# Gate projections of a three-layer stack: one weight load for both activation halves, blocks of 256 channels, the forget-gate attention's gate multiplied later

## The chip, the cores and the metric

The kernel runs on one NeuronCore of one Trainium2 chip. The metric is the device time of one execution in microseconds. All arrays lie in HBM before the start and the result is written back there.

## The reference

A stack of three layers over 256 tokens of width 2048, in float32. Layers 0 and 1 share one form. Each modulates and normalises `x` to `u`, projects `u` with `w_in` (2048 by 19064), runs three branches and merges them. What matters here, cut down:

```python
proj = jnp.dot(u, w_in)
(fq, fk, fv, ff, fg, dq, dk, dv, iq, ik, iw, dg, sz, sxbc, sdt, mg) = jnp.split(proj, ...)
y_fox = fox_attention(fq, fk, fv, log_f).reshape(B, S, FOX_WIDTH) * jax.nn.silu(fg)
y_dsa = dsa_attention(dq, dk, dv, iq, ik, iw).reshape(B, S, DSA_WIDTH) * jax.nn.silu(dg)
y_ssd = ...            # state-space branch, times silu(sz), grouped rms_norm
gates = jax.nn.sigmoid(mg.reshape(B, S, 3, D) + b_merge)
merged = (gates[:, :, 0] * jnp.dot(y_fox, w_o_fox) + gates[:, :, 1] * jnp.dot(y_dsa, w_o_dsa)
          + gates[:, :, 2] * jnp.dot(y_ssd, w_o_ssd))
x = x + gate[:, None, :] * jnp.dot(merged, w_out)
# third layer (layer 2 in the kernel)
y_a = h.astype(x.dtype) * jax.nn.silu(g_lru)
y_b = windowed_gqa(q, k, v, sink) * jax.nn.silu(g_attn)
```

The gate blocks of the title are the projections to `fg` and `dg` (1024 channels each, in layers 0 and 1) and to `g_lru` and `g_attn` (2048 channels each, in layer 2).

## The kernel before

**Products.** Each large product is done with float32 operands split in a high part and a low part: `UH`, `UL` for `u`; `HH`, `LL` for a piece of weights. Three products are summed in PSUM: high by high, low activation by high weight, high activation by low weight. A piece of weights is 1 MB (128 partitions by 2048 words), called a chunk. Its way is: a DMA to one of the `RAW` buffers; `hi` on ScalarE (L1511), which writes `HH`; `lo` on VectorE (L1875), which writes `LL` over the RAW buffer; then the products on TensorE (L1277). There are 3 `HH` buffers, so `hi` of chunk g waits until the products of chunk g - 3 are done, and ScalarE, which works strictly in order, waits with it.

**Blocks.** A block is 512 output channels, that is 4 chunks of 4 k-tiles of 128 rows. Blocks use two sets of two PSUM banks in turn (set 0: `G0`, `G1`; set 1: `G2`, `G3`), so block n + 2 can begin only when block n is evacuated. There are two kinds. In kind `tm` (tokens by channels) the activations are the loaded operand and 512 columns of weights stream: 24 matmuls of 512 columns a chunk. In kind `cm` (channels by tokens) the weights are loaded and 256 columns of activations stream: 48 matmuls of 256 columns a chunk. The profile names a matmul by the streamed operand and then the loaded one, `G<-UH,HH`. The gate blocks are `cm`: 4 blocks each in layers 0 and 1 and 8 in layer 2, 16 in all.

**Order.** `work_order` makes one list of tokens, and each engine's program walks it and takes its own. After the products of each chunk it calls `slot`, which takes one step of the side lane (attention, state-space scan, recurrences, tables for the next layer) and one step of the evacuation lane (a first-in-first-out queue of block evacuations and of the splits of `y` into `YH`, `YL`). If the block about to start needs a set whose last block has no evacuation step yet, `gemm` calls `slot` again until it has, with no products in between; what is put then stands behind the `hi` of the chunk two places further on. A block marked `ahead` has the pending `lo` put before its evacuation step. Chunks are numbered in this order; chunks 93 to 100 are the `fg` blocks of layer 0, 294 to 297 the last four of them in layer 1.

**Gates.** A gate block's evacuation is `silu` (two tokens, one a bank): ScalarE takes tanh of the bank into `S1` (L1617), VectorE makes (tanh + 1) times the bank (L2062) and multiplies this into the attention's or recurrence's result, `QQ` or `XS` (L2069). It is held until that result is there. Before `fg` come four `sz` blocks, whose evacuation takes more steps: `sz_gate` (tanh on ScalarE L1655, two operations on VectorE L2100 and L2103, once for each bank), `sz_norm` (L1659, L1661, L2109, L2111), a turn on TensorE (L1372) and `sz_put` (L2116). After the `fg` blocks come the gates of the merge (`gate`, L2127 and L1675), the splits (L1690, L2156) and, in layer 1, tables of layer 2: `rope` (L1917 to L1939, sine L1552) and `lru_par` (L2195 to L2258, L1732, L1735). `ada` is a dot product on VectorE (L1886, two of 128x1024).

## Time and profile before

| | |
|---|---|
| time, median of 3 runs | 3382.77 us (3380.96 to 3383.23) |
| profiled execution, first to last instruction | 3380.1 us |
| median less that span (start and end around it) | 2.7 us |
| TensorE busy | 3279.9 us, 97% of the span |
| VectorE busy | 2253.8 us, 67% |
| ScalarE busy | 1690.3 us, 50% |
| mean granted clock of TensorE | 0.992 |

A row of a timeline reads: start in us from the span's start, duration, engine, line, operation, output <- inputs, count; in brackets the idle time of that engine before it and what ended it. PE is TensorE, DVE is VectorE, ACT is ScalarE. A matmul's duration is its time through the array; consecutive ones overlap, so what a matmul costs in a stream is the distance from its start to the next start.

### The profile page before, as it was taken

Reading aid. Unit: us, or ns where it says so; the run is one execution under the profiler, and the core shown is the slowest. Engines: PE = TensorE matmul, PEld = TensorE weight load, DVE = VectorE, ACT = ScalarE, POOL = GpSimd, SP = SyncE. Lnnn points to the kernel's source line nnn. Section 1 sums busy time; section 2 is a strip of 40 time slices with the busy share of each in tenths; the row PEclk is TensorE's granted clock in tenths of the full one; section 3 lists DMA queues with packets and bytes.
Section 4 is the critical chain, followed back from the end, with each engine's and each line's share of the span. In section 5 each row is a group of like instructions: output and inputs, shape, how many; then the busy total and the mean of one; then the engine's idle time right before and its main releaser. Section 6 shows DMA issues by size and latency. Waiting matters only on the chain.

```text
span 3380.1 us, 43397 instructions
## 1 busy us (share of the span) xinstructions
PE 3279.9 (97%) x17994; PEld 2845.1 (84%) x17994; DVE 2253.8 (67%) x2699; ACT 1690.3 (50%) x2090; POOL 46.8 (1%) x90
## 2 busy tenths in 40 slices
PE   4899999999999999999999999999999999999998
PEld 3789889888888878898898888888798899988887
DVE  7878878866676556786666676655577776544454
ACT  4455764643433445556646544334447865434343
POOL 0000000000000000000000000000000000000000
PEclk8999999999999999999999999999999999999999
DMA  9854566567777654444544577765545443455554
GB/s 403 325 187 174 200 252 252 197 232 273 270 278 277 227 206 175 175 152 175 185 175 164 185 264 268 277 220 190 196 183 191 181 165 131 174 213 198 188 188 147
DMA packets 102916, 719.29 MB, mean 213 GB/s; under 512 B 12176, under 2 KB 12256, under 8 KB 18752
## 3 DMA queue, kind: packets, MB, share of 16 engines
q1 hardware_dynamic: 93888, 675.38, 54.0%
q0 software_dynamic: 8256, 37.64, 3.1%
q8 instruction: 142, 2.33, 0.3%
q10 hardware_dynamic: 576, 3.50, 0.3%
q14 instruction: 54, 0.44, 0.0%
HBM read 710.08 MB, written 6.40 MB: 212 GB/s over the span
## 4 chain that ended last, share of the span: by engine, by line
PE 88%; DVE 7%; DMA 2%; ACT 2%; issue 1%; DVEq 0%; ACTq 0%
PE G L1277 81%; DVE LL L1875 2%; DMA RAW<-w_ada_turned_packed_dram 2%; PE BD L1389 1%; DVE S L2079 1%; PE BA L1416 1%; DVE RAW L1868 1%; PE BD L1451 1%; DMA KV<-in_x_dram 1%; PE BC L1402 0%; PE BE L1332 0%; DVE RAW L1886 0%; PE BA L1470 0%; PE BC L1470 0%; PE BC L1434 0%
## 5 line engine op out<-in xcount | busy, mean ns | idle before, releaser
L1511 ACT ACTIVATE HH<-RAW 128x2048 fp32r<-128x2048 f32 x546 | 1044.8, 1914 | 1096.7 <-PE G L1277 1019.1
L1875 DVE TENSOR_TENSOR LL<-RAW,HH 128x2048 fp32r<-128x2048 f32 x546 | 1248.0, 2287 | 370.5 <-ACT HH L1511 370.0
L1277 PE MATMUL G<-HH,UH 128*128 128x512 f32 x2496 | 994.2, 398 | 35.1 <-DVE LL L1875 23.4
L1277 PE MATMUL G<-LL,UH 128*128 128x512 f32 x2496 | 977.0, 391 | 0.0
L1277 PE MATMUL G<-HH,UL 128*128 128x512 f32 x2496 | 976.7, 391 | 0.0
L1277 PE MATMUL G<-UH,HH 128*128 128x256 f32 x2080 | 602.0, 289 | 5.7 <-DVE LL L1875 5.6
L1277 PE MATMUL G<-UH,LL 128*128 128x256 f32 x2080 | 588.8, 283 | 0.0
L1277 PE MATMUL G<-UL,HH 128*128 128x256 f32 x2080 | 588.7, 283 | 0.0
L1277 PEld LDWEIGHTS G<-HH,UH 128*128 128x128 f32 x2496 | 471.7, 189 | 137.4 <-DVE LL L1875 26.1
L1277 PEld LDWEIGHTS G<-LL,UH 128*128 128x128 f32 x2496 | 471.4, 189 | 100.4
L1277 PEld LDWEIGHTS G<-HH,UL 128*128 128x128 f32 x2496 | 471.7, 189 | 97.9 <-issue 2.9
L1277 PEld LDWEIGHTS G<-UH,HH 128*128 128x128 f32 x2080 | 398.9, 192 | 12.2 <-DVE LL L1875 8.0
L1277 PEld LDWEIGHTS G<-UL,HH 128*128 128x128 f32 x2080 | 399.2, 192 | 1.8 <-issue 1.0
L1277 PEld LDWEIGHTS G<-UH,LL 128*128 128x128 f32 x2080 | 398.9, 192 | 0.0
L1277 PE MATMUL G<-HH,YH 128*128 128x512 f32 x768 | 299.9, 391 | 0.0
L1277 PE MATMUL G<-LL,YH 128*128 128x512 f32 x768 | 299.0, 389 | 0.0
L1277 PE MATMUL G<-HH,YL 128*128 128x512 f32 x768 | 298.8, 389 | 0.0
L1277 PEld LDWEIGHTS G<-LL,YH 128*128 128x128 f32 x768 | 144.2, 188 | 30.1
L1277 PEld LDWEIGHTS G<-HH,YH 128*128 128x128 f32 x768 | 144.2, 188 | 29.9 <-DVE LL L1875 0.3
L1277 PEld LDWEIGHTS G<-HH,YL 128*128 128x128 f32 x768 | 144.2, 188 | 29.7
L1886 DVE SCALAR_TENSOR_TENSOR RAW<-RAW,CH 128x1024 f32<-128x1024 f32 x128 | 151.3, 1219 | 0.0
L2079 DVE SCALAR_TENSOR_TENSOR S<-G,PAR,S 128x253 f32<-128x253 f32 x144 | 69.3, 481 | 42.5 <-ACT S L1631 38.2
(387 smaller groups left out, 2329.0 us busy)
## 6 DMA issues: line engine op xcount, KB each, us to landing
RAW<-in_w_in_packed_dram SPq DMA_DIRECT2D x402, 1024.0 KB, 4.8
RAW<-w_ada_turned_packed_dram SPq DMA_DIRECT2D x96, 1024.0 KB, 5.0
RAW<-in_w_out_packed_dram SPq DMA_DIRECT2D x48, 1024.0 KB, 4.8
...
```

The lines of the kernel that those rows point to most:

```text
L1277: mm = pe.matmul(to, lt, rh, start=first, stop=end, skip_group_check=True)
L1389: mm = pe.matmul(BD[:, j * P:(j + 1) * P], vt[:, t, vof(h + j):vof(h + j) + P], W[3][:, (j * nt + t) * P:(j * nt + t + 1) * P], start=t == ...
L1416: mm = pe.matmul(to, QQ[:, h + j, qt * P:(qt + 1) * P], kt[:, kof(h + j), 0:nk], start=True, stop=True)
L1451: pe.matmul(BD[:, j * 64:(j + 1) * 64], W[j // 4][:, (j % 4) * P:(j % 4 + 1) * P], XD[:, j * 64:(j + 1) * 64], start=True, stop=True)
L1511: a.activation(HH[g % NH][:, :n], RAW[buf(ch["f"])][:, :n], ACT.Copy).then_inc(*hi_done.up(g))
L1868: v.scalar_tensor_tensor(RAW[buf(f)][:, :], RAW[buf(f)][:, :], 0.5, CB[:, :], ALU.mult, ALU.mult, accum_out=DOT[:, 0, c:c + 1]).then_inc(* ...
L1875: v.tensor_tensor(LL[buf(f)][:, :n], RAW[buf(f)][:, :n], HH[g % NH][:, :n].bitcast(F32), ALU.subtract).then_inc(*lo_done.up(g))
L1886: done = v.scalar_tensor_tensor(r, r, 0.5, CH[:, :], ALU.mult, ALU.mult, accum_out=DOT[:, e["half"], c:c + 1])
L2079: v.scalar_tensor_tensor(to, of, weight(j), to, ALU.mult, ALU.add).then_inc(*done.up(*key, n))
```

## The change

A gate block is now 256 channels: 2 chunks of 8 k-tiles (`wide`). `UH` and `UL` become the two halves of one tile `UU`, side by side for each k-tile. For each k-tile and each 128 channels there are two matmuls instead of three on each 256 columns: the high weights are loaded once and stream 512 columns, high and low activations, into the whole bank; the low weights stream the 256 high columns into its first half. The sum of the two halves of the bank is then left to the evacuation. This `sg` copies the first half to SBUF on ScalarE, adds the second half on VectorE (this frees the bank), takes tanh of the sum on ScalarE and multiplies on VectorE. A second token, `sm`, multiplies by the result of the attention or recurrence. For `dg`, `gl` and `ga` `sm` follows `sg`; for `fg` the gates stay in `BT` and `CTT` (free once the state-space branch is done) and `times_late` multiplies them after all four blocks.

```diff
+    def wide(self, w, c0, evac, ready, **kw):
+        chunks = []
+        for kc in range(KT // 8):
+            src = (*w, kc * 1024, 1024, [(c0, 256)])
+            parts = [("ab", j, 0, j * P, P, 0) for j in range(2)]
+            chunks.append({"src": src, "w": 256, "nk": 8, "k0": kc * 8, "parts": parts})
+        return self.block(chunks, evac, ("U", 0), ready, KT, **kw)
...
+    def silu_gate(key, prog):
         def steps(b):
             o.tok_block[key] = b
-            for j in range(2):
-                put("silu", key, j)
+            put("sg", key)
+            o.blocks[b]["free_by"] = ("sg_sum", key)
+            ended("sg_silu", key)
+            yield
+            yield from times(key, prog)
+        return steps
+
+    def silu_early(key, prog):
+        def steps(b):
+            o.tok_block[key] = b
+            while not prog["done"]:
                 yield
-            ended("silu_done", key, 1)
+            put("sg", key)
+            o.blocks[b]["free_by"] = ("sg_sum", key)
+            ended("sg_silu", key)
+            yield
         return steps
...
-        for j in range(2):
-            o.wblock(w, DG + j * 512, o.held(o.att_prog["dsa", l][j], silu_times(("dg", l, j))), u_ready, ahead=True)
+        for j in range(4):
+            o.wide(w, DG + j * 256, silu_gate(("dg", l, j), o.att_prog["dsa", l][j // 2]), u_ready, ahead=True)
...
-            add_to(s_fd, [split(("y", l, i)) for i in range(4)])
+            add_to(s_fd, [times_late(l)] + [split(("y", l, i)) for i in range(4)])
...
-        for j in range(2):
-            o.wblock(w, FG + j * 512, o.held(o.att_prog["fox", l][j], silu_times(("fg", l, j))), u_ready, ahead=True,
-                     after=after_fg if j else None)
+        for j in range(4):
+            o.wide(w, FG + j * 256, silu_early(("fg", l, j), o.ssd_prog[l][3]), u_ready, ahead=True,
+                   after=after_fg if j == 3 else None)
...
-    UH = sb("UH", [P, KT, S], F32R)
-    UL = sb("UL", [P, KT, S], F32R)
+    UU = sb("UU", [P, KT, 2, S], F32R)
+    UH, UL = UU[:, :, 0, :], UU[:, :, 1, :]
...
-                for j in range(3):
+                for j in range(2 if kind == "ab" else 3):
...
+                    if kind == "ab":
+                        w_ = (hv, lv)[j]
+                        end = kk == b["kts"] - 1 and j == 1
+                        to = GB[b["set"]][bi][:, 0:(512, S)[j]]
+                        lt, rh = w_[:, k, c0:c0 + P], (UU[:, kk, :, :].rearrange("p a b -> p (a b)"), UH[:, kk, :])[j]
...
+            for j in range(2):
+                i = a.activation(g[:, j, :], GB[o.blocks[b]["set"]][j][:, 0:S], ACT.Copy)
+            i.then_inc(*sg_copied.up(key))
+            a.wait_ge(*sg_sum.at(key))
+            a.activation(th, g, ACT.Tanh, scale=0.5).then_inc(*sg_tanh.up(key))
...
+            for j in range(2):
+                i = v.tensor_tensor(g[:, j, :], g[:, j, :], GB[o.blocks[b]["set"]][j][:, S:2 * S], ALU.add)
+            i.then_inc(*sg_sum.up(key))
+            v.wait_ge(*sg_sum.at(key))
+            v.wait_ge(*sg_tanh.at(key))
+            v.scalar_tensor_tensor(g, th, 1.0, g, ALU.add, ALU.mult).then_inc(*sg_silu.up(key))
```

**Place 1, ScalarE, layer 0, from the `hi` of chunk 96 on.** `HH` numbers are the chunk number modulo 3; `L1655` is the tanh of `sz_gate`, here of the last `sz` block. Before:

```order
L1511 ACTIVATE HH0<-RAW0 128x2048
L1511 ACTIVATE HH1<-RAW1 128x2048
L1655 ACT_TABLE_LOAD
L1655 ACTIVATE S1<-G2 128x512
L1511 ACTIVATE HH2<-RAW3 128x2048
L1655 ACTIVATE XD<-G3 128x512
L1659 ACTIVATE S1,SM2<-XS 128x512
```

Now (the lines are 52 to 57 further down: L1563 is `hi`, L1712 the tanh of `sz_gate`, L1671 and L1674 the copies and the tanh of `sg`):

```order
L1563 ACTIVATE HH0<-RAW0 128x2048
L1563 ACTIVATE HH1<-RAW1 128x2048
L1712 ACT_TABLE_LOAD
L1712 ACTIVATE S1<-G2 128x512
L1712 ACTIVATE XD<-G3 128x512
L1716 ACTIVATE S1,SM2<-XS 128x512
L1718 ACT_TABLE_LOAD
```

Both `sz_gate` steps now stand directly behind the `hi` of chunk 97, and TensorE's chunk 95, the first of the second `fg` block, which takes `G2` and `G3`, waits for both; before, chunk 95 was in the middle of a block that already had its banks.

**Place 2, VectorE, layer 0, a little later.** `L1886` and `L1944` are `ada`, `L2116` and `L2180` are `sz_put`, `LL` rows are `lo`. Before, up to the first `silu` of `fg`, which the chunk after the `fg` blocks waits behind:

```order
L2116 TENSOR_TENSOR XS<-BE,PAR 128x512
L1875 TENSOR_TENSOR LL1<-RAW1,HH2 128x2048
L1875 TENSOR_TENSOR LL2<-RAW2,HH0 128x2048
L2062 SCALAR_TENSOR_TENSOR S1<-S1,G0 128x512
L2069 SCALAR_TENSOR_TENSOR QQ<-S1,QQ 128x512
L1875 TENSOR_TENSOR LL4<-RAW4,HH1 128x2048
L2062 SCALAR_TENSOR_TENSOR S1<-S1,G1 128x512
L2069 SCALAR_TENSOR_TENSOR QQ<-S1,QQ 128x512
```

Now (L1933 is `lo`, L2118 the add of `sg`):

```order
L1944 SCALAR_TENSOR_TENSOR RAW2,DOT<-RAW2,CH 128x1024 x2
L2180 TENSOR_TENSOR XS<-BE,PAR 128x512
L1933 TENSOR_TENSOR LL3<-RAW3,HH2 128x2048
L2180 TENSOR_TENSOR XS<-BE,PAR 128x512
L1933 TENSOR_TENSOR LL4<-RAW4,HH0 128x2048
L2118 TENSOR_TENSOR BT<-BT,G0 128x256
L2118 TENSOR_TENSOR BT<-BT,G1 128x256
L2122 SCALAR_TENSOR_TENSOR BT<-S1,BT 128x512
```

The adds that free `G0` and `G1` for chunk 97 (the third `fg` block) stand behind the `lo` of chunk 99 (`LL4<-RAW4,HH0`), whose `hi` waits for the end of chunk 96. The wait at the end of the `fg` blocks, behind `LL4<-RAW4,HH1` (chunk 103) in the rows of before, has gone: there the adds stand two blocks earlier.

**Place 3, ScalarE, layer 1, after the `fg` blocks.** `YH<-QQ` are the four splits, `ROWS` and `SPL` the two steps of `lru_par`, `WW` the tanh of the first merge gate. Before:

```order
L1511 ACTIVATE HH2<-RAW5 128x2048
L1735 ACT_TABLE_LOAD
L1735 ACTIVATE SPL<-PAR 128x32
L1690 ACTIVATE YH<-QQ 128x1024
L1511 ACTIVATE HH0<-RAW0 128x2048
L1690 ACTIVATE YH<-QQ 128x1024
L1511 ACTIVATE HH1<-RAW2 128x2048
L1690 ACTIVATE YH<-QQ 128x1024
L1675 ACT_TABLE_LOAD
L1675 ACTIVATE WW<-WW 128x512 x2
L1511 ACTIVATE HH2<-RAW3 128x2048
```

Now (L1748 the split, L1793 `SPL`, L1732 the tanh of the merge gate):

```order
L1563 ACTIVATE HH0<-RAW0 128x2048
L1790 ACT_TABLE_LOAD
L1790 ACTIVATE ROWS<-ROWS 128x32
L1748 ACTIVATE YH<-QQ 128x1024
L1563 ACTIVATE HH1<-RAW2 128x2048
L1793 ACT_TABLE_LOAD
L1793 ACTIVATE SPL<-PAR 128x32
L1748 ACTIVATE YH<-QQ 128x1024 x2
L1732 ACT_TABLE_LOAD
L1732 ACTIVATE WW<-WW 128x512 x2
L1563 ACTIVATE HH2<-RAW3 128x2048
```

Behind the `hi` of chunk 304 (`HH1<-RAW2`) stood one split and the gate's tanh; now `SPL`, two splits and the gate's tanh stand there.

## Rows read from the trace of the kernel before

**Rows 1.** The page: busy time, then the chain that ended last.

```profile
PE 3279.9 (97%) x17994; PEld 2845.1 (84%) x17994; DVE 2253.8 (67%) x2699; ACT 1690.3 (50%) x2090; POOL 46.8 (1%) x90
...
PE 88%; DVE 7%; DMA 2%; ACT 2%; issue 1%; DVEq 0%; ACTq 0%
```

**Rows 2.** Timeline of TensorE inside a `cm` chunk: first and 48th matmul.

```profile
530.02 0.28 PE L1277 MATMUL G<-UH,HH 128*128 128x256 f32 x1
...
535.66 0.28 PE L1277 MATMUL G<-UH,LL 128*128 128x256 f32 x1
```

**Rows 3.** Timeline of TensorE in a `tm` chunk: first and 20th matmul shown.

```profile
2219.63 0.39 PE L1277 MATMUL G<-LL,YH 128*128 128x512 f32 x1
...
2223.94 0.39 PE L1277 MATMUL G<-HH,YH 128*128 128x512 f32 x1
```

**Rows 4.** Timeline of TensorE at the end of `fg`, layer 0.

```profile
723.55 0.28 PE L1277 MATMUL G<-UH,LL 128*128 128x256 f32 x1
729.63 0.77 PE L1277 MATMUL G<-HH,UH 128*128 128x512 f32 x1 [5.80 <-DVE QQ L2069]
...
732.72 0.40 PE L1277 MATMUL G<-HH,UL 128*128 128x512 f32 x1
```

**Rows 5.** The same place: timelines of ScalarE (one row) and VectorE.

```profile
723.93 1.91 ACT L1511 ACTIVATE HH<-RAW 128x2048 fp32r<-128x2048 f32 x1 [1.93 <-PE G L1277]
...
725.87 2.29 DVE L1875 TENSOR_TENSOR LL<-RAW,HH 128x2048 fp32r<-128x2048 f32 x1 [2.13 <-ACT HH L1511]
...
728.79 0.69 DVE L2069 SCALAR_TENSOR_TENSOR QQ<-S,QQ 128x512 f32<-128x512 f32 x1
```

**Rows 6.** Timeline of TensorE, layer 1: the same wait, and the one after the splits.

```profile
1916.79 0.77 PE L1277 MATMUL G<-HH,UH 128*128 128x512 f32 x1 [5.80 <-DVE QQ L2069]
...
1952.56 0.50 PE L1277 MATMUL G<-HH,UH 128*128 128x512 f32 x1 [0.98 <-DVE LL L1875]
```

**Rows 7.** `sz_gate` of the last `sz` block, layer 0: timelines of ScalarE and VectorE.

```profile
688.47 1.92 ACT L1511 ACTIVATE HH<-RAW 128x2048 fp32r<-128x2048 f32 x1 [4.27 <-PE G L1277]
690.40 1.28 ACT L1655 ACT_TABLE_LOAD   x1
691.70 0.60 ACT L1655 ACTIVATE S<-G 128x512 f32<-128x512 f32 x1
...
693.05 0.69 DVE L2103 SCALAR_TENSOR_TENSOR XS<-S,XS 128x512 f32<-128x512 f32 x1
```

**Rows 8.** By line: a copy and an operation near 256 columns, and `ada`.

```profile
L1760 ACT ACTIVATE QQ<-BD x48: 358/384/385, 379.5 to 2906.1; 128x256 f32<-128x256 f32 x48
...
L2079 DVE SCALAR_TENSOR_TENSOR S<-G,PAR,S 128x253 f32<-128x253 f32 x144 | 69.3, 481 | 42.5 <-ACT S L1631 38.2
...
L1886 DVE SCALAR_TENSOR_TENSOR RAW<-RAW,CH 128x1024 f32<-128x1024 f32 x128 | 151.3, 1219 | 0.0
```

**Rows 9.** Timelines of layer 1 after `fg`: ScalarE, then VectorE.

```profile
1940.65 1.92 ACT L1511 ACTIVATE HH<-RAW 128x2048 fp32r<-128x2048 f32 x1 [1.00 <-PE G L1277]
1943.22 1.06 ACT L1690 ACTIVATE YH<-QQ 128x1024 fp32r<-128x1024 f32 x1 [0.66 <-DVE YL L2156]
...
1940.27 0.17 DVE L2205 TENSOR_SCALAR PAR<-PAR 128x32 f32<-128x32 f32 x1
...
1941.97 1.22 DVE L2156 SCALAR_TENSOR_TENSOR YL<-QQ,YH 128x1024 fp32r<-128x1024 f32 x1
1943.11 2.29 DVE L1875 TENSOR_TENSOR LL<-RAW,HH 128x2048 fp32r<-128x2048 f32 x1
...
1950.22 2.28 DVE L1875 TENSOR_TENSOR LL<-RAW,HH 128x2048 fp32r<-128x2048 f32 x1
```

**Rows 10.** Stretch with `dg` blocks, layer 0: PE, PEld, DVE, ACT, POOL busy.

```profile
540.00:560.00 20.00, 20.00 (x165) 19.52 (x165) 17.64 (x24) 8.10 (x11) 0.00 (x0) 1.00 0.69 259
```

**Rows 11.** Layer 2, after a `ga` evacuation: timelines of VectorE and TensorE.

```profile
2910.89 2.28 DVE L1875 TENSOR_TENSOR LL<-RAW,HH 128x2048 fp32r<-128x2048 f32 x1
...
2914.49 0.28 PE L1277 MATMUL G<-UH,HH 128*128 128x256 f32 x1
```

More of the change, by code:

```diff
@@ L429, in tokens, with times, times_late @@
         return steps
-    def silu_times(key):
+    def silu_gate(key, prog):
         def steps(b):
             o.tok_block[key] = b
-            for j in range(2):
-                put("silu", key, j)
+            put("sg", key)
[8 more added lines that the diff above has]
+            while not prog["done"]:
                 yield
-            ended("silu_done", key, 1)
-        return steps
+            put("sg", key)
+            o.blocks[b]["free_by"] = ("sg_sum", key)
+            ended("sg_silu", key)
+            yield
+        return steps
+    def times(key, prog):
+        while not prog["done"]:
+            yield
+        put("sm", key)
+        ended("sm_done", key)
+        yield
+    def times_late(l):
+        for j in range(4):
+            while not o.att_prog["fox", l][j // 2]["done"]:
+                yield
+            put("sm", ("fg", l, j))
+            ended("sm_done", ("fg", l, j))
+            if j % 2:
+                yield
     def conv(l, jb):
@@ L795, in work_order @@
     o.side.add(o.when(qkv_b, attention("att2", 2)))
-    for j in range(4):
-        o.wblock(w, 2048 + j * 512, o.held(lru_prog[j], silu_times(("gl", 2, j))), u_ready2)
+    for j in range(8):
+        o.wide(w, 2048 + j * 256, silu_gate(("gl", 2, j), lru_prog[j // 2]), u_ready2)
     s_a, s_b, s_u2 = [], [], []
@@ L805, in after_gates @@
         add_to(s_a, [split(("a", 2, i)) for i in range(4)] + [bring(2)])
-    for j in range(4):
-        o.wblock(w, 7168 + j * 512, o.held(o.att_prog["att2", 2][j], silu_times(("ga", 2, j))), u_ready2,
-                 after=after_gates if j == 3 else None)
+    for j in range(8):
+        o.wide(w, 7168 + j * 256, silu_gate(("ga", 2, j), o.att_prog["att2", 2][j // 2]), u_ready2,
+               after=after_gates if j == 7 else None)
     branch(2, 0, w, 9216, ("w_proj_a_2", 0), 0, 16, lambda kk: ("split_lo", ("a", 2, kk // 4)), s_a, u_ready2,
@@ L1046, in hybrid_stack @@
     dv_copied = count("dv_copied", [(h[1], t) for h, t in o.all("hd") if h[0] == "dk"])
-    silu_tanh = count("silu_tanh", o.all("silu"))
-    silu_done = count("silu_done", o.all("silu"))
+    sg_copied, sg_sum = count("sg_copied", o.all("sg")), count("sg_sum", o.all("sg"))
+    sg_tanh, sg_silu = count("sg_tanh", o.all("sg")), count("sg_silu", o.all("sg"))
+    sm_done = count("sm_done", o.all("sm"))
     sz_tanh, sz_y = count("sz_tanh", o.all("sz_gate")), count("sz_y", o.all("sz_gate"))
@@ L1567, in u @@
                 a.wait_ge(*u_full.at(l, pi))
[L1568 removed]
+                a.activation(UH[:, 2 * pi:2 * pi + 2, :], SS[pi % 2][:, :].rearrange("p (a b) -> p a b", a=2),
+                             ACT.Copy).then_inc(*u_hi.up(l, pi))
         def gate_cols(l):
@@ L2053, in hd, with sg, sm @@
                 rotated.append((h, t))
-        def silu(key, j):
+        def sg(key):
             b = o.tok_block[key]
-            bk = GB[o.blocks[b]["set"]][j]
-            dst, c0 = silu_dst[key[0]]
-            c0 += key[2] * 4 + 2 * j
-            d = flat(dst[:, c0:c0 + 2, :])
-            v.wait_ge(*silu_tanh.at(key, j))
-            v.scalar_tensor_tensor(S1[:, :], S1[:, :], 1.0, bk[:, :], ALU.add, ALU.mult).then_inc(*own.up())
-            v.wait_ge(*own.last())
+            g, th = gate_tiles(key)
+            v.wait_ge(*sg_copied.at(key))
+            for j in range(2):
[4 more added lines that the diff above has]
+            v.scalar_tensor_tensor(g, th, 1.0, g, ALU.add, ALU.mult).then_inc(*sg_silu.up(key))
+        def sm(key):
+            dst, c0 = silu_dst[key[0]]
+            d = dst[:, c0 + 2 * key[2]:c0 + 2 * key[2] + 2, :]
+            v.wait_ge(*sg_silu.at(key))
             if key[0] == "gl":
-                v.wait_ge(*lru_done.at(key[2] * 4 + 3))
+                v.wait_ge(*lru_done.at(2 * key[2] + 1))
             else:
                 name = {"dg": "dsa", "fg": "fox", "ga": "att2"}[key[0]]
-                v.wait_ge(*att_y.at(name, key[1], key[2] * 4 + 3))
-            v.scalar_tensor_tensor(d, S1[:, :], 0.5, d, ALU.mult, ALU.mult).then_inc(*silu_done.up(key, j))
+                v.wait_ge(*att_y.at(name, key[1], 2 * key[2] + 1))
+            v.scalar_tensor_tensor(d, gate_tiles(key)[0], 0.5, d, ALU.mult, ALU.mult).then_inc(*sm_done.up(key))
         def taps(done, main, key, ps, dst, weight, shifts):
```

36 lines of the change are left out of this document (21 added, 15 removed).

## The prediction, written before the changed kernel was run

> **What bounds the kernel now.** The page comes first: TensorE is busy 97% of the span and holds 88% of the chain that ended last, while VectorE has 67% and ScalarE 50% [rows 1]. So a change pays in two ways only: cheaper matmul streams, or fewer and shorter holes on TensorE. For the streams I read TensorE's timeline. Inside a `cm` chunk 48 starts lie between 530.02 and 535.66, 0.120 us apart [rows 2]; in a `tm` chunk 20 starts span 4.31 us, 0.227 us apart [rows 3]. At 2.4 GHz, the level of both stretches, 256 columns are 0.1067 us and 512 are 0.2133 us, so a matmul with its load costs its columns and 0.0133 us more, at either size. For the holes I read the same timeline at the ends of blocks. The largest inside the layers stands at the end of `fg`: last start at 723.55, next at 729.63, 5.96 us more than a step of the stream, and again in layer 1 [rows 4, 6]. The row names VectorE's `QQ` as what ended it. The chain back is: end of chunk 100, `hi` at 723.93 (0.38 us after that last start), `lo` at 725.87, the two `silu` operations until 729.48, TensorE 0.15 us later [rows 5]. After it the clock is at its lower level until 732.72: seven matmuls take 3.09 us where the stream needs 1.59, a loss of 1.5 us [rows 4].
>
> **The streams.** The 16 gate blocks hold 16 x 4 chunks x 48 = 3072 matmuls of 256 columns. They become 1024 of 512 and 1024 of 256 columns. The columns are the same; 1024 matmuls and loads go, at 0.0133 us each: -13.7 us. A chunk takes 16 x 0.347 = 5.55 us instead of 5.76. No row shows a 256-column matmul between two of 512 with other weights, so the bounds are: nothing saved, if the extra time comes back where the sizes alternate, and twice the row, -27 us, if the 256-column ones also lose theirs. I take the row's figure, as both sizes show the same excess.
>
> Here a page speaks against the gain. The Trainium skill, "TensorE: Matmul & The Clock Gate" (section "Wait — 56ns, not 53.3ns?"), says that back-to-back matmuls at full clock start their columns at 2.4 GHz plus about 2.5 ns apart. By that floor the 1024 removed would give 2.6 us and the sum below would be +23.7, where the row gives +12.6. The rows differ from it: 13.3 ns here, with a load before each matmul, and the row decides.
>
> **The old hole.** The adds of the last `fg` blocks stand early enough, so 5.96 us go in each of two layers: -11.9 us. Its clock loss goes with it, and comes back below.
>
> **New hole A** (place 1 of the change), both layers. The `fg` blocks are half as long, but the evacuation of the last `sz` block needs as many steps. Chunk 95 is now the first of a block that needs the banks of that `sz` block, and both `sz_gate` steps stand behind the `hi` of chunk 97, which waits for the end of chunk 94. From the last start of chunk 94: `hi` at +0.38; by the spacings of rows 7 table load at +2.31, first tanh at +3.61, second operation of VectorE at +4.96, ending at +5.65; the second bank's tanh is done by then, its two operations take 0.69 each and 0.03 between, to +7.06; TensorE at +7.21, 7.1 us beyond a step [rows 5, 7]. Nothing hides it: the next products need that bank. 2 x 7.1 = +14.2 us. The clock will fall as after the old hole: 2 x 1.5 = +3.0 us.
>
> **New hole B** (place 2), both layers. Chunk 97 waits for the adds of the first `fg` block, behind the `lo` of chunk 99, whose `hi` waits for the end of chunk 96. `hi` +0.38 to +2.30, `lo` to +4.6, two adds of 256 columns. The nearest row for one is an operation of 253 columns at 0.481 us, between nothing (an add hidden in the wait) and 0.69 us, that of 512 columns [rows 5, 7, 8]; I take 0.45, so +5.5, TensorE at +5.65: 5.5 us each, +11.0 us. Its clock loss replaces that of the old hole.
>
> **Hole C** (place 3), layer 1. Before, chunk 304 started 1.1 us late at 1952.56, as soon as its `lo` of 1950.22 had ended [rows 6, 9]; that `lo` stands behind the merge gate's two adds and an `ada`. Counted from the end of chunk 301 (about 1940.3) the chain was: `hi` 304, third split's low part with a `lo` of 2.29 us behind it, last split, add, `ada` (2.44), add, `lo`. Now that `lo` is ahead of the chain, but in it come the third split's high part (1.05) and low part (1.22), a table load (1.28) with the small steps of `lru_par` (0.3 before the split, and 1.70 as between 1940.27 and 1941.97) [rows 7 to 9]. In order: `hi` to +2.2, table +3.5, `SPL` +4.2, high part +5.2, low +6.4, `lru_par` +8.1, low part of the last split +9.3, add +10.1, `ada` +12.4, add +13.0, `lo` +15.3. Two `tm` chunks last 10.9, so chunk 304 is 4.4 us late by that. ScalarE and VectorE also come later to this point, since the sines and an `ada` now stand behind the last `sg`: counted in the same way from the start of chunk 298 (add, tanh, two `lo`, two `sm`, `ada`, sines at 2.5 and 2.0 us, estimated from the ten small steps), `lo` of chunk 302 ends at +23.2 where TensorE wants it at +21.9, 1.3 us late, and the `hi` of 304 and VectorE's own `lo` of 303 come about 1.4 us late against the products. Sum 7.1 us against 1.1: +6.0 us, and a loss of clock, +1.5 us. If all of `lru_par` hides in idle time this is +2.
>
> **VectorE in `dg` of layer 0.** A 512-channel pair of blocks costs VectorE 4 adds x 0.45 and 4 operations x 0.69, 4.6 us, against 2.7 before; so +3.6 us for the four blocks, and each `sg` waits about 0.7 us for ScalarE's tanh (0.60) besides: 6.4 us in all over eight chunks, some 48 us. VectorE has 2.4 us idle in 20 there, so 5.7 in that time [rows 8, 10]. It becomes the limit: the 1.7 us that these chunks save are lost and about 0.5 more: +2.2 us. In layer 1 and elsewhere VectorE has room.
>
> **Layer 2.** With no attention beside it, the `lo` two chunks on followed a `ga` evacuation at 2910.89 and ended at 2913.17, 1.3 us before its matmul at 2914.49 [rows 11]. `sg` is longer by one copy step and the wait for tanh, about 1 us, and the chunk is 0.2 shorter: the margin is 0.1 us. I count +0.3 us for all of it. ScalarE's copies are 0.38 us each against a tanh of 0.60 and hide [rows 7, 8].
>
> **Sum:** -13.7 - 11.9 + 14.2 + 3.0 + 11.0 + 7.5 + 2.2 + 0.3 = +12.6 us. The profiled span is 3380.1 us, with 2.7 us around it to the median of 3382.77: the span becomes 3392.7 and the time 3395.4, 0.37% slower. What a measurement of this kernel can tell from no change is about 0.2%, 6.8 us: 3376.0 to 3389.6.
>
> **Rivals.**
> *The holes are shallow (same).* If the clock does not fall at A and C and C costs 2 us, the sum is 12.6 - 3.0 - 5.5 = +4.1: 3387 us. For it: a hole of 5.96 us cost 1.5, not more, and phases vary. Against it: both old holes of that length show the loss. Chance 0.18.
> *The loads are worth more (faster).* If the 13 ns go from the 256-column matmuls too, -27 instead of -13.7, the time is 3382; with shallow holes as well 3374, faster. With my holes it turns at a saving of 33 us. For it: no row of mixed sizes. Against: both sizes carry the same excess. Chance of both together: 0.05.
> *VectorE becomes the limit in layer 2 as well (slower still).* If each of the 16 wide blocks there loses 1 us because margins of 1.3 us are too short, +16: 3411 us. It decides from 1.3 us of added delay at each `sg`. Against: beside attention a chunk lasts longer and margins are wider. Chance 0.12.
> *The streams give little (slower still).* If the excess over the columns belongs to a change of weights that cannot be hidden, and the alternation of sizes costs it again, 2.6 us or less come instead of 13.7: 3406 us. For it: no row alternates. Against: the excess is the same behind 256 and 512 columns. Chance 0.07. The page named above gives this time.
> *The change costs nothing and gives the loads alone.* If A does not stand where the order puts it, 3395.4 - 14.2 - 3.0 = 3378. Against: bank and order are fixed in the program. Chance 0.05.
>
> **Numbers.** Forecast as summed 0.53, own range 3390 to 3401. Faster: the 0.05 of the load rival and 0.02 from the rival without hole A, 0.07. Same: 0.18 and the other 0.03, less 0.01 that ends above 3389.6, 0.20. Slower: 0.53 + 0.12 + 0.07 + 0.01, 0.73. The range for 8 in 10 goes from 3384 (shallow holes, adds hidden) to 3404 (a third of the layer-2 rival).
>
> **What would show it.** Starts 0.227 and 0.120 us apart in turn inside a wide chunk, 5.55 us a chunk. No hole at the first merge-gate chunk after `fg`. A hole of about 7 us ended by VectorE's `XS` (`sz_gate`) before the second `fg` block, one of 5.5 ended by the add into `BT` before the third, each twice, with a lower clock behind. A wait of some 6 us on `lo` at chunk 304. Wrong would make it: a start distance other than 0.347 a pair, or TensorE waiting at every wide block.

## The result and the profile after

The changed kernel takes 3398.15 us (median of 4 runs, 3396.97 to 3400.08) against 3382.77 for the kernel before: a ratio of 1.0047, with a 95% interval of 1.0033 to 1.0062. It is 0.47% slower, where +12.6 us, 0.37%, was forecast. The profiled execution has a span of 3395.2 us, 15.1 more than before.

The page of the changed kernel, with the rows that answer to [rows 1], and from its costliest groups the one that holds the wide blocks' first products, with the idle time of TensorE just before them:

```profile
PE 3276.9 (97%) x16970; PEld 2795.5 (82%) x16970; DVE 2276.1 (67%) x2763; ACT 1707.3 (50%) x2152; POOL 46.6 (1%) x90
...
PE 85%; DVE 8%; DMA 2%; ACT 2%; issue 1%; DVEq 0%; POOL 0%; ACTq 0%; POOLq 0%
...
L1329 PE MATMUL G<-UU,HH 128*128 128x256 f32 (+1 forms) x3136 | 765.7, 327 | 30.6 <-DVE XS L2167 13.7
```

1024 matmuls are gone (17994 to 16970). The busy time says nothing of what that gave, since it counts slow stretches too; the last row does: TensorE stood idle 30.6 us before these products, 13.7 of them for `XS`, which `sz_gate` writes. That is hole A, 6.83 us in each of the two layers. Timeline of TensorE in the changed kernel, at A (two rows), at B (two rows) and within a wide chunk (the last four):

```profile
685.23 0.28 PE L1329 MATMUL G<-UU,LL 128*128 128x256 f32 x1
692.34 0.77 PE L1329 MATMUL G<-UU,HH 128*128 128x512 f32 x1 [6.83 <-DVE XS L2167]
...
705.37 0.28 PE L1329 MATMUL G<-UU,LL 128*128 128x256 f32 x1
...
710.79 0.77 PE L1329 MATMUL G<-UU,HH 128*128 128x512 f32 x1 [4.70 <-DVE BT L2118]
...
718.70 0.39 PE L1329 MATMUL G<-UU,HH 128*128 128x512 f32 x1
718.93 0.28 PE L1329 MATMUL G<-UU,LL 128*128 128x256 f32 x1
719.04 0.39 PE L1329 MATMUL G<-UU,HH 128*128 128x512 f32 x1
...
724.13 0.28 PE L1329 MATMUL G<-UU,LL 128*128 128x256 f32 x1
```

From last start to next start A is 7.11 us and B 5.42; in layer 1 they are the same (1878.13 to 1885.24, 1899.00 to 1904.42). Nothing is left of the old hole [rows 4, 6]: the chunk that it preceded starts 0.12 us after the last start of the one ahead of it. This wide chunk has 32 starts in 5.43 us, where 48 took 5.64 [rows 2]; others take 5.53, as the part on the streams tells. Behind A, ScalarE (three rows) and VectorE (four) show the chain that was forecast, and behind B the `lo` with the two adds (last two rows):

```profile
685.61 1.91 ACT L1563 ACTIVATE HH<-RAW 128x2048 fp32r<-128x2048 f32 x1 [4.07 <-PE G L1329]
687.53 1.28 ACT L1712 ACT_TABLE_LOAD   x1
688.83 0.60 ACT L1712 ACTIVATE S<-G 128x512 f32<-128x512 f32 x1
...
689.46 0.69 DVE L2164 SCALAR_TENSOR_TENSOR S<-S,G 128x512 f32<-128x512 f32 x1 [5.59 <-ACT S L1712]
...
691.50 0.69 DVE L2167 SCALAR_TENSOR_TENSOR XS<-XD,XS 128x512 f32<-128x512 f32 x1
...
707.68 2.29 DVE L1933 TENSOR_TENSOR LL<-RAW,HH 128x2048 fp32r<-128x2048 f32 x1 [0.87 <-ACT HH L1563]
709.90 0.74 DVE L2118 TENSOR_TENSOR BT<-BT,G 128x256 f32<-128x256 f32 x2
```

Windows of the changed kernel over the chunks behind A and B in layer 0, then over the next chunk for comparison, then behind A and B in layer 1 (length; busy time and count of PE, PEld, DVE, ACT, POOL; then the granted clock, 1.00 being 2.4 GHz throughout, the DMA share and GB/s):

```profile
692.30:699.30 7.00, 6.96 (x32) 6.06 (x33) 5.71 (x8) 1.83 (x5) 0.00 (x0) 0.79 0.00 0
710.70:718.60 7.90, 7.81 (x32) 6.78 (x33) 4.42 (x8) 1.89 (x4) 0.00 (x0) 0.68 0.00 1
718.70:724.20 5.50, 5.50 (x34) 4.85 (x33) 2.29 (x1) 1.92 (x1) 0.00 (x0) 1.00 0.76 286
1885.20:1893.00 7.80, 7.76 (x32) 6.75 (x33) 3.50 (x5) 1.83 (x5) 0.00 (x0) 0.70 0.01 2
1904.40:1912.70 8.30, 8.28 (x32) 7.13 (x33) 2.14 (x4) 1.82 (x4) 0.00 (x0) 0.64 0.00 0
```

From its first to its last start the four chunks behind the holes take 6.93, 7.80, 7.67 and 8.27 us instead of 5.43. The loss is 8.9 us; 6.0 was forecast (twice 1.5 behind A, twice 1.5 behind B).

Hole C stands at chunk 304, with six chunks of products between it and `fg` in layer 1. TensorE of the changed kernel there, then VectorE's last operations ahead of it:

```profile
1962.80 0.39 PE L1329 MATMUL G<-LL,YH 128*128 128x512 f32 x1
1968.69 1.22 PE L1329 MATMUL G<-HH,UU 128*128 128x512 f32 x2 [5.50 <-DVE LL L1933]
...
1960.28 0.35 DVE L2274 RECIPROCAL PAR<-PAR 128x32 f32<-128x32 f32 x1
...
1961.44 1.22 DVE L2220 SCALAR_TENSOR_TENSOR YL<-QQ,YH 128x1024 fp32r<-128x1024 f32 x1
...
1965.75 0.69 DVE L2191 TENSOR_TENSOR WW<-G,S 128x512 f32<-128x512 f32 x1
1966.35 2.28 DVE L1933 TENSOR_TENSOR LL<-RAW,HH 128x2048 fp32r<-128x2048 f32 x1
```

5.89 us between starts, ended by `lo`, with `lru_par`'s small operations (the `RECIPROCAL` is one), the last split and the merge gate ahead of it; the chunk behind it takes 6.84 us against 5.21.

The times at which chunks start on TensorE cut the span into stretches. The table gives their lengths in us from the traces of four kernels (e9 and e10, the last experiments below, are the changed kernel and the kernel before in a better order), and the change of each stretch from before to after as forecast (sums of the terms that fall into it) and as measured:

| chunks | what | before | after | forecast | measured | e10 | e9 |
|---|---|---|---|---|---|---|---|
| 69-77 | `dg`, layer 0 | 52.0 | 51.3 | +0.5 | -0.7 | 52.0 | 51.3 |
| 77-93 | up to `fg` | 113.4 | 111.8 | 0 | -1.7 | 112.3 | 112.3 |
| 93-101 | `fg`, layer 0, with the old hole, A, B | 54.3 | 62.6 | +7.9 | +8.2 | 48.2 | 47.6 |
| 101-105 | first merge chunks | 23.3 | 21.8 | -1.5 | -1.5 | 21.8 | 21.8 |
| 262-290 | `dg` and `sz`, layer 1 | 179.3 | 177.9 | -1.7 | -1.4 | 179.8 | 178.4 |
| 290-298 | `fg`, layer 1, with the old hole, A, B | 53.4 | 62.9 | +7.9 | +9.5 | 47.0 | 46.2 |
| 298-306 | merge, with C | 46.8 | 51.8 | +6.0 | +5.0 | 43.6 | 45.6 |
| 434-450 | `gl`, layer 2 | 109.9 | 109.9 | -3.1 | 0.0 | 109.9 | 109.8 |
| 450-466 | `ga`, layer 2 | 114.5 | 112.2 | -3.4 | -2.3 | 114.5 | 111.8 |

### The profile page after: what moved, and what is told of

It is laid out like the page before. It is cut to its first block, busy times and chain, and to the rows that moved or that the text cites. A ratio compares the mean times of both kernels' runs of the same rounds, so it can differ in the third digit from the quotient of the medians.

```text
span 3395.2 us, 41523 instructions
## 1 busy us (share of the span) xinstructions
PE 3276.9 (97%) x16970; PEld 2795.5 (82%) x16970; DVE 2276.1 (67%) x2763; ACT 1707.3 (50%) x2152; POOL 46.6 (1%) x90
## 3 DMA queue, kind: packets, MB, share of 16 engines
q1 hardware_dynamic: 93888, 675.38, 54.3%
## 4 chain that ended last, share of the span: by engine, by line
PE 85%; DVE 8%; DMA 2%; ACT 2%; issue 1%; DVEq 0%; POOL 0%; ACTq 0%; POOLq 0%
PE G L1329 79%; DVE LL L1933 3%; DMA RAW<-w_ada_turned_packed_dram 2%; PE BD L1441 1%; DVE S L2143 1%; PE BA L1468 1%; PE BD L1503 1%; DVE RAW L1926 1%; DVE RAW L1944 1%; ACT HH L1563 1%; PE BC L1454 0%; PE BE L1384 0%; PE BC L1486 0%; PE BA L1522 0%; PE BC L1522 0%
## 5 line engine op out<-in xcount | busy, mean ns | idle before, releaser
L1329 PE MATMUL G<-HH,UU 128*128 128x512 f32 x4992 | 1563.5, 395 | 27.6 <-DVE LL L1933 27.4
L1563 ACT ACTIVATE HH<-RAW 128x2048 fp32r<-128x2048 f32 x546 | 1044.5, 1913 | 1040.8 <-PE G L1329 977.7
L1933 DVE TENSOR_TENSOR LL<-RAW,HH 128x2048 fp32r<-128x2048 f32 x546 | 1248.1, 2287 | 364.6 <-ACT HH L1563 364.0
L1329 PEld LDWEIGHTS G<-HH,UU 128*128 128x128 f32 x4992 | 934.4, 189 | 227.2 <-DVE LL L1933 30.5
L1329 PE MATMUL G<-LL,UU 128*128 128x512 f32 x2496 | 976.5, 391 | 0.0
L1329 PE MATMUL G<-UU,HH 128*128 128x256 f32 (+1 forms) x3136 | 765.7, 327 | 30.6 <-DVE XS L2167 13.7
L1329 PEld LDWEIGHTS G<-UU,HH 128*128 128x128 f32 x3136 | 526.5, 192 | 83.7 <-DVE LL L1933 20.4
L1329 PE MATMUL G<-UU,LL 128*128 128x256 f32 x2080 | 589.3, 283 | 0.0
L1329 PEld LDWEIGHTS G<-LL,UU 128*128 128x128 f32 x2496 | 470.6, 189 | 99.6
L1329 PEld LDWEIGHTS G<-UU,LL 128*128 128x128 f32 x2080 | 400.4, 193 | 1.6 <-issue 1.0
L1944 DVE SCALAR_TENSOR_TENSOR RAW<-RAW,CH 128x1024 f32<-128x1024 f32 x128 | 151.3, 1219 | 0.0
L2191 DVE TENSOR_TENSOR WW<-G,S 128x512 f32<-128x512 f32 x48 | 33.0, 689 | 75.9 <-PE G L1329 75.5
L1926 DVE SCALAR_TENSOR_TENSOR RAW<-RAW,CB 128x2048 f32<-128x2048 f32 x32 | 72.9, 2288 | 7.3 <-DMA RAW<-w_ada_turned_packed_dram 7.2
```

Source lines behind the costliest of these rows:

```text
L1329: mm = pe.matmul(to, lt, rh, start=first, stop=end, skip_group_check=True)
L1563: a.activation(HH[g % NH][:, :n], RAW[buf(ch["f"])][:, :n], ACT.Copy).then_inc(*hi_done.up(g))
L1926: v.scalar_tensor_tensor(RAW[buf(f)][:, :], RAW[buf(f)][:, :], 0.5, CB[:, :], ALU.mult, ALU.mult, accum_out=DOT[:, 0, c:c + 1]).then_inc(* ...
L1933: v.tensor_tensor(LL[buf(f)][:, :n], RAW[buf(f)][:, :n], HH[g % NH][:, :n].bitcast(F32), ALU.subtract).then_inc(*lo_done.up(g))
L1944: done = v.scalar_tensor_tensor(r, r, 0.5, CH[:, :], ALU.mult, ALU.mult, accum_out=DOT[:, e["half"], c:c + 1])
L2191: v.tensor_tensor(GT[:, t, :], GB[o.blocks[b]["set"]][t][:, :], BIAS[:, :], ALU.add).then_inc(*gate_add.up(key, t))
```

## The experiments

**Two sz gates in one step.** Theory: the loss is the place of a few instructions. Rival: the three-part evacuation is too much for VectorE, and the holes only show where.

```diff
     def sz(l, g):
...
             put("sz_gate", l, g, 0)
-            yield
             put("sz_gate", l, g, 1)
```

The changed kernel with it:

> The changed kernel with one edit: the two gate operations of an sz bank pair stand in one step of the order, so that the last sz evacuation takes four steps and ends before the chunks that need its banks and its ScalarE and VectorE places. Theory (the loss of the change is the place of a few instructions in the order: holes A and B behind the last sz block, and the lower clock behind each): the holes of 7.1 and 5.4 us at the second and third fg block vanish in both layers, 2 x (7.0 + 5.3) = 24.6 us, and with them the clock losses of 8.7 us in all; hole C in layer 1 stays. 3398.2 - 33 = 3365 us, from 3361 to 3371. Rival (the new evacuation in three parts, with ScalarE's copies and a wait for tanh, is itself too much for VectorE and ScalarE, and the holes are only where that shows): the holes move to another chunk of the fg blocks, and the time falls by less than 8 us, 3390 us or more.

3379.32 us, ratio to before 0.9989 (0.9981 to 0.9998): 18.8 us less than the changed kernel, not 33. The kernel before with it:

> The kernel before with the same edit as the run above: both gate operations of an sz bank pair in one step. It gives the like-for-like value of the change: the change itself is worth this run against the run above. Theory: the old hole at the end of fg (5.96 us in each layer) was also a matter of the late sz evacuation, which pushed the silu operations of the last fg block back; it goes in both layers with its clock losses of 1.5 us each, less 1 to 2 us in the merge branch of layer 1: 3382.8 - 13 = 3370 us, from 3366 to 3373, some 5 us above the run above. Rival (the old hole is due to the silu evacuation of 512 channels as such): the hole stays, 3380 us or more, and the wide blocks then have a merit of their own of 15 us.

3384.92 us, 1.0007 (0.9999 to 1.0016): no gain. The first time lies between the ranges of theory and rival. The second is the rival's figure, 3380 or more, though the hole that the rival wanted to stay is gone. The traces show why: A, B and the old hole are gone in both (`fg` takes 47.1 and 48.4 us in layer 0), but the edit also touched the first three `sz` blocks, beside attention, and there both kernels lost some 7 to 9 us in layer 0 (chunks 77 to 93: 120.3 and 120.2 us) and 4.6 in layer 1. TensorE of the first of the two kernels, the largest new wait:

```profile
635.71 1.09 PE L1423 MATMUL BE<-CST,XS 128*128 128x128 f32 x4 [4.38 <-DVE XS L2179]
```

Transposes of `sz` wait for VectorE's add of the ones before, since they now come one step earlier while VectorE works on attention and `ada`; the 24 products of the chunk behind them (with attention's matmuls among them) take 9.4 us from first to last start against 7.2. So the theory holds for the holes and the edit was too wide. Like for like, that is with the same edit in both kernels, the change is worth -5.6 us here.

**Three products again.** What do 1024 fewer loads give?

```diff
-                for j in range(2 if kind == "ab" else 3):
+                for j in range(3):
...
                     if kind == "ab":
...
-                        to = GB[b["set"]][bi][:, 0:(512, S)[j]]
-                        lt, rh = w_[:, k, c0:c0 + P], (UU[:, kk, :, :]..., UH[:, kk, :])[j]
+                        to = GB[b["set"]][bi][:, (0, S, 0)[j]:(0, S, 0)[j] + S]
+                        lt, rh = w_[:, k, c0:c0 + P], x_[:, kk, :]
```

> The changed kernel with one edit: the products of the wide blocks are again three matmuls of 256 columns with a weight load each (high weights x high half, high x low half, low x high half) in place of one of 512 and one of 256 columns; blocks of 256 channels, evacuation and order stay as changed. Theory (the load that goes with each matmul costs 13.3 ns, so 1024 of them 13.7 us, of which layer 0's dg blocks and layer 2 realised only a part because other engines set the pace there): +8 to +13 us, 3406 to 3411 us; a chunk of these blocks takes 5.76 us again instead of 5.55. Rival (the Trainium skill's floor of about 2.5 ns for back-to-back matmuls): 1024 x 2.5 ns = 2.6 us, 3401 us.

3407.26 us, 1.0071 (1.0058 to 1.0084): 9.1 us more than the changed kernel, inside the theory's range. The two profiled executions differ by 10.2 us, of which 1.6 lie at chunk 89, which the edit leaves alone: the clock in it was 1.00 in the changed kernel and 0.81 here. TensorE of this kernel, first matmuls and last of a wide chunk:

```profile
723.57 0.40 PE L1327 MATMUL G<-UU,HH 128*128 128x256 f32 x2
...
729.21 0.28 PE L1327 MATMUL G<-UU,LL 128*128 128x256 f32 x1
```

5.64 us again, against 5.43. The 0.21 us for 16 matmuls is 13 ns each in this chunk; in others it is half of that, as the part on the streams tells. The Trainium skill, "TensorE: Matmul & The Clock Gate" (section "Wait — 56ns, not 53.3ns?"), has 2.5 ns for starts back to back; this case, with a load for each matmul, shows more than five times that.

Since only the products differ, this run also parts what the loads give from what the new evacuation costs. With three products `dg` of layer 0 takes 52.0 us, `dg` and `sz` of layer 1 179.3 and `ga` 114.5, as in the kernel before: the evacuation costs nothing there, and the loads give 0.7, 1.4 and 2.3 us. `gl` takes 111.4 against 109.9: there the evacuation costs 1.5 us.

**`fg` as before.** 512-channel blocks, `silu` in the evacuation; `dg`, `gl` and `ga` stay wide.

```diff
-        for j in range(4):
-            o.wide(w, FG + j * 256, silu_early(("fg", l, j), o.ssd_prog[l][3]), ...)
+        for j in range(2):
+            o.wblock(w, FG + j * 512, o.held(o.att_prog["fox", l][j], silu_times(("fg", l, j))), ...)
```

> The changed kernel with one edit: the forget-gate blocks of both layers are as before (512 channels a block, three products, silu in the evacuation and multiplied into the attention there, nothing kept for later); dg, gl and ga stay wide. Theory (all the loss sits in the fg blocks and what they move: A, B, the clock behind them, the added part of C): no holes A and B, the old hole of 5.96 us at the end of fg back in both layers, chunk 304 some 1 us late as before; the wide blocks left give 0.7 us in dg of layer 0, 1.4 in dg of layer 1 and 2.3 in layer 2, as measured between the two kernels. 3382.8 - 4.4 = 3378 us, from 3375 to 3381. Rival (the wide blocks lose by their evacuation wherever they stand): 3386 us or more.

3377.03 us, 0.9981 (0.9972 to 0.9990), as the theory had it. TensorE shows the old hole and no A or B:

```profile
730.61 0.76 PE L1340 MATMUL G<-HH,UU 128*128 128x512 f32 x1 [5.80 <-DVE QQ L2143]
```

So all of the loss, 21.1 us against the changed kernel, comes with `fg`; elsewhere the change gives 5.7.

**Only the last two sz blocks.** First the gates alone:

```diff
             put("sz_gate", l, g, 0)
-            yield
+            if g < 2:
+                yield
             put("sz_gate", l, g, 1)
```

> The changed kernel, with the two gate operations of an sz bank pair in one step for the third and fourth sz block only. With all four (the first experiment) some 9 us were lost in the sz blocks of layer 0 and 6 in those of layer 1, where transposes came to wait for VectorE (4.5 us at 630.9). Here the first two blocks stay as they were, and the gate operations of the last sz block stand ahead of the hi of chunk 97, but the sum of the first fg block still behind the hi and lo of chunk 99. Theory (each hole belongs to one instruction behind one hi): hole A goes in both layers, 14.0 us and the clock loss of the one chunk behind it (1.5 and 2.1 us); hole B stays with 5.4 us and its clock loss; C stays; up to 3 us come in the merged sz block. 3398.2 - 17.6 = 3380.6 us, from 3378 to 3385. Rival (A and B are one shortage of VectorE that only moves): B grows by what A loses, 3393 us or more.

3383.57 us, 1.0003 (0.9994 to 1.0012): 14.6 less than the changed kernel, in the theory's range. TensorE at the places of A and B:

```profile
688.83 0.47 PE L1330 MATMUL G<-UU,HH 128*128 128x512 f32 x1 [1.29 <-DVE XS L2168]
...
705.85 0.77 PE L1330 MATMUL G<-UU,HH 128*128 128x512 f32 x1 [4.70 <-DVE BT L2119]
```

A shrinks from 6.83 to 1.29 us of idle, B keeps its 4.70 to the hundredth. They are two waits, not one shortage. Then the same in the transposes' adds, which puts B's sum one step earlier too:

```diff
             put("sz_turn", l, g, 1)
-            yield
+            if g < 2:
+                yield
             put("sz_put", l, g, 1)
```

> As the run above, and in the third and fourth sz block the second transpose's add also stands in the step of the first, so that these two blocks take three steps each and the sum of the first fg block stands ahead of the hi of chunk 99. Theory: A and B both go, 24.6 us and 8.7 us of clock, and 2 to 4 us come in the sz blocks; C stays. 3398.2 - 33.3 + 3 = 3368 us, from 3364 to 3373. Rival (holes only move with the shortage): 3385 us or more.

> The kernel before with the same edit of the sz steps as the run above, to have the change's own worth with the holes of both kernels gone. Theory: the old hole of 5.96 us goes in both layers with 1.5 us of clock each, 2 to 4 us come in the sz blocks and up to 4 at chunk 304 of layer 1, whose lo now stands behind lru_par as in the changed kernel: 3382.8 - 15 + 6 = 3374 us, from 3370 to 3379, some 6 us above the run above (as the two runs with all four sz blocks merged: 3384.9 against 3379.3). Rival (the wide blocks have a cost of their own at the end of the layers): no more than 2 us between the two.

The changed kernel takes 3369.43 us with it (0.9962, 0.9948 to 0.9976), the kernel before 3371.24 (0.9964, 0.9952 to 0.9977). Both lie in their ranges, but the two differ by 1.8 us, not by 6. No more than 2 us between them was the rival of the second run, that the wide blocks have a cost of their own at the end of the layers, and the traces show two such costs: in layer 0 a wait of 2.7 us is left before chunk 97, and C has its full 5.6 us where the kernel before has 3.9.

**Splits one step earlier, `lo` first in layer 2.**

```diff
 def times_late(l):
...
             ended("sm_done", ("fg", l, j))
-            if j % 2:
-                yield
+        yield
...
-        o.wide(w, 2048 + j * 256, silu_gate(("gl", 2, j), lru_prog[j // 2]), u_ready2)
+        o.wide(w, 2048 + j * 256, silu_gate(("gl", 2, j), lru_prog[j // 2]), u_ready2, ahead=True)
```

(and the same `ahead` for `ga`)

> The changed kernel with the sz steps of e6, and two more edits: the four late multiplications of fg stand in one step of the order, so the splits behind them come one step earlier and the lo of chunk 304 in layer 1 has only one split ahead of it that is not yet needed; and in layer 2 the lo of a chunk stands ahead of the evacuation of the wide blocks. Theory: hole C falls from 5.9 us to about 1.1 to 3 us with or without its clock loss of 1.6 (minus 3 to 6.4), and the waits of 1.1 and 1.0 us at chunks 440 and 442 go (minus 2): 6 us less than e6, about 3362 us, from 3358 to 3368. Rival (the order does not matter there, since VectorE and ScalarE have the same work to do before chunk 304): C as long as in e6, and lo ahead of sg makes the sums late instead: the same as e6 or slower.

3373.26 us, 0.9971 (0.9960 to 0.9983): 3.8 slower than e6. The theory fell, and the rival's "the same as e6 or slower" came true. C lost 1.1 us, but the four multiplications in one step put the `lo` of chunk 301 behind them, and TensorE waited 2.0 us there and 0.3 more at 302: chunks 298 to 306 last as long as in e6 (+0.06). In `gl` two waits of 1.1 us became one of 2.1. The two profiled executions differ by 3.0 us, and they do so where the edits change nothing: +1.9 in chunks 93 to 101 and +1.5 in 105 to 262, with -0.4 in 290 to 298. The first is the clock (1.6), and a slower spacing of the starts behind it (0.3). Windows from 699 to 709 us of e8 and then of e6:

```profile
699.00:709.00 10.00, 7.43 (x34) 6.14 (x33) 7.42 (x10) 3.61 (x5) 0.00 (x0) 0.83 0.29 105
```

```profile
699.00:709.00 10.00, 7.43 (x43) 6.35 (x42) 7.42 (x10) 4.08 (x6) 0.00 (x0) 1.00 0.29 105
```

The same wait, 2.73 us beyond a step, lies in both; the clock fell behind it in one and not in the other.

**Layer 2's parameters later.** What else stands between what chunk 304 needs is work that nothing needs yet: the sines (`rope`) and `lru_par`.

```diff
     def load_second():
         put("rows", 2)
-        yield
-        yield
+        for _ in range(10):
+            yield
         yield from rope(2)
...
-            o.wide(w, FG + j * 256, silu_early(...), u_ready, ahead=True,
+            o.wide(w, FG + j * 256, silu_early(...), u_ready, ahead=j > 0,
```

The second edit is only in the wide kernel. All three runs have the sz steps of e6.

> The changed kernel with the sz steps of e6; the sines and the parameters of layer 2 (rope and lru_par) are put into the order eight steps later, behind the merge branch's first two blocks, and in each layer the lo of the chunks two on stands behind, not ahead of, the sum of the first fg block (and of the second in layer 1). Theory (hole C is the sines and lru_par between what chunk 304 needs): the hole of 5.9 us at chunk 304 and the 1.0 us at 302 shrink to 1 to 2 us in all, and the lower clock behind them goes (1.6); the 2.7 us before chunk 97 fall to about 1. 3369.4 - 4.5 - 1.6 - 1.5 = 3362 us, from 3359 to 3366. Rival (C comes from the late multiplications and splits, and the moved work only waits elsewhere): 3368 us or more.

> The kernel before with the sz steps of e7 and rope and lru_par of layer 2 eight steps later, as in the run above. Theory: the 3.9 us before chunk 304 go to 1 or less, and what is lost to the clock behind them (1.6): 3371.2 - 5 = 3366 us, from 3364 to 3369, so that the wide blocks are worth 2 to 6 us like for like. Rival: no gain here, 3370 us or more.

> As the run above (sz steps and late parameters), with dg, gl and ga in wide blocks and fg as before, in blocks of 512 channels. It parts what the wide blocks are worth in fg from the rest, in an order with few holes. Theory (the wide blocks of dg, gl and ga realise 4.4 us, as in e4, and those of fg in an order without holes save 16 x 0.21 = 3.4 us each layer pair, less 1 to 2 us at chunk 97 and in the splits): this run is 4 to 5 us below the run above and 0 to 3 above e9, 3362 us, from 3359 to 3365. Rival (fg kept for later costs more than its streams save even here): below e9 by 2 us or more.

| | us | ratio to before |
|---|---|---|
| e9, all gate blocks wide | 3360.52 | 0.9937 (0.9925 to 0.9950) |
| e10, kernel before | 3365.20 | 0.9953 (0.9940 to 0.9967) |
| e11, `fg` as before, others wide | 3360.82 | 0.9938 (0.9926 to 0.9951) |

All three as the theory had it. e9's group of the wide blocks' first products, its wait at chunk 304, and its window that holds both fg holes of the changed kernel, which had 44.47 us of PE busy and a clock of 0.88 in the same window:

```profile
L1331 PE MATMUL G<-UU,HH 128*128 128x256 f32 (+1 forms) x3136 | 757.0, 324 | 8.6 <-DVE LL L1935 7.8
...
1934.87 0.74 PE L1331 MATMUL G<-HH,UU 128*128 128x512 f32 x2 [1.72 <-DVE LL L1935]
...
684.00:740.00 56.00, 55.27 (x297) 47.31 (x296) 42.98 (x48) 28.25 (x30) 1.60 (x3) 1.00 0.71 266
```

Idle before those products fell from 30.6 to 8.6 us. e9 is 22 us faster than the kernel before; 17.3 of that the order alone gives (e10), and the change's own worth is the 4.7 between e10 and e9, which the two intervals do not part by themselves. It is not quite like for like either, as only e9 has the second edit: the wait of 2.7 us before chunk 97, which only the wide kernel had, is 0.5 in e9. In the traces the difference is 4.7 as well, and it comes from `dg` (0.7 and 1.4 us in the two layers) and `ga` (2.7). It does not come from `fg`, whose blocks save 0.6 and 0.8 us and give 2.1 back in chunks 298 to 306; e11 has `fg` as before and takes the same time as e9.

## Why the prediction was right

**The streams (-13.7).** Right in kind, too large in size: the term that was mis-sized is the saving for each load, 0.0133 us in every wide chunk. The starts do alternate, but at one of two spacings, and a chunk mostly keeps to one. Of the 64 wide chunks of the changed kernel 23 have the forecast 0.347 us a pair and end 0.21 us sooner than three products do; 38 have 0.353 us a pair and end about 0.10 sooner; in the other three the clock is down for most of the chunk. First starts and last of chunk 463, in `ga`, with nothing beside the products on TensorE:

```profile
2929.88 0.40 PE L1329 MATMUL G<-UU,HH 128*128 128x512 f32 x1
2930.11 0.28 PE L1329 MATMUL G<-UU,LL 128*128 128x256 f32 x1
2930.22 0.40 PE L1329 MATMUL G<-UU,HH 128*128 128x512 f32 x1
...
2935.41 0.28 PE L1329 MATMUL G<-UU,LL 128*128 128x256 f32 x1
```

5.53 us against the 5.43 of chunk 98, both at a clock of 1.00. 23 chunks at the full saving and 38 at half of it (16 loads each) make 9.0 us; e3 measures 9.1, and 13.7 was forecast. The prediction had named a start distance other than 0.347 a pair as a sign of being wrong, and it holds in more than half of the chunks: part of the excess came back with the alternation, as its rival of the cheap streams had it, but not all. `ga` gives 2.3 of 3.4 by this, `dg` of layer 0 0.7 of 1.7; in the latter chunk 74 takes 0.3 us longer besides, and no run tells why.

**The old hole (-11.9), A (+14.2), B (+11.0).** Right in place, chain and size: 2 x 5.96 gone, 2 x 6.99 and 2 x 5.3 come (7.11 and 5.42 less a step). B is 0.2 shorter each because an add of 256 columns takes 0.37 us, half of the 0.74 above, not 0.45. e5 and e6 show the cause: moving one instruction ahead of one `hi` takes most of one hole away and leaves the other as it was, and moving a second takes the other but for 2.7 us in layer 0.

**The clock behind the holes (+3.0, B's for the old one's).** Mechanism right, size too small: 8.9 us come behind A and B. What goes is 1.5 us in layer 0 and 1.8 in layer 1, where the first chunk after the old hole took 7.05 us against 5.21; the forecast had read layer 0 alone. That makes +5.6. The clock was 0.73 and 0.74 in the chunks behind the two old holes, and 0.79, 0.68, 0.70 and 0.64 in the four here.

**C (+6.0, and 1.5).** Right: 0.80 us beyond a step at chunk 302 (1.3 forecast) and 5.66 at 304 (5.8), less the 1.1 of before, with 1.6 us of clock. e9 and e10 show the cause that was argued: with the sines and `lru_par` out of the chain, the kernel before has no wait left there and the wide one 1.9 us. That the late multiplications push the splits is part of it too, but packing them closer moved the wait instead of removing it (e8).

**VectorE as the limit in `dg` of layer 0 (+2.2).** Wrong: TensorE waits for no `lo` there. The stretch became 0.7 us shorter, each `lo` there ended 2.0 us or more before its product, and with three products (e3) the new evacuation left the stretch at the 52.0 us of before. Window of the changed kernel:

```profile
515.50:569.10 53.60, 53.46 (x309) 45.69 (x308) 45.46 (x60) 27.77 (x45) 0.83 (x2) 1.00 0.62 236
```

VectorE is busy 45.5 of 53.6 us (43.2 of 54.3 in the kernel before), so the added work of `sg` fitted. Its waits for ScalarE were counted as work that TensorE has to wait for, while `lo` ended some 3 us ahead of most chunks and could take them up.

**Layer 2 (+0.3).** Too small: the margin of 1.3 us was read after a `ga` evacuation [rows 11] and taken for all of layer 2. In `gl`, beside the recurrence, ScalarE was already busy 20.7 us in 32 before the change, and `sg` waits for it. Window of the kernel before, then VectorE of the changed kernel, and TensorE's two waits:

```profile
2733.00:2765.00 32.00, 32.00 (x259) 31.68 (x259) 24.76 (x30) 20.72 (x21) 0.00 (x0) 1.00 0.47 165
...
2765.79 0.75 DVE L2118 TENSOR_TENSOR S<-S,G 128x256 f32<-128x256 f32 x2 [1.91 <-ACT S L1671]
2767.30 0.69 DVE L2122 SCALAR_TENSOR_TENSOR S<-S 128x512 f32<-128x512 f32 x1 [0.77 <-ACT S L1674]
2767.91 2.28 DVE L1933 TENSOR_TENSOR LL<-RAW,HH 128x2048 fp32r<-128x2048 f32 x1
...
2770.25 0.50 PE L1329 MATMUL G<-UU,HH 128*128 128x512 f32 x1 [0.93 <-DVE LL L1933]
...
2777.04 0.51 PE L1329 MATMUL G<-UU,HH 128*128 128x512 f32 x1 [0.87 <-DVE LL L1933]
```

VectorE stands idle 1.91 and 0.77 us inside one `sg`, with the `lo` behind it. It is the rival of a limit in layer 2 in small: 4.2 us more than forecast in `gl` and `ga` together, not 16. The two waits are 1.8 of the 4.2 (2.1 against 0.3); the rest is the slower spacing.

**The sum.** In the trace +15.1 against +12.6: +4.2 in layer 2, +2.6 of clock behind the holes, -0.4 for B, -0.7 for C, -1.2 in `dg` of layer 0 (the limit of 2.2 that was not there, less 1.0 of saving that did not come), -1.7 in chunks 77 to 93. In the last the kernel before had a slower chunk behind the wait at 643.7 us (clock 0.81), and the changed one, with the same wait, did not (1.00). A and small pieces make the remainder of -0.3. So the places and sizes of the holes were foreseen, but that the total came within 3 us is in part luck: loads that gave 4.6 less and 2.6 of clock went one way, the limit in `dg` and the chunk that no edit touches the other. The rivals: the shallow holes are refuted by the four chunks behind A and B, the cheap streams and the dearer loads by the 9.1 us of e3, which lie between the 2.6 of the one and the 27 of the other, the missing hole A by its 7.11 us.
